# Three mixed sequence blocks in one kernel: other order of half slabs, sums, loads and banks around the first ups of two MLPs

## The reference

```python
# block 2
hdn = jnp.square(jax.nn.relu(rms_norm(x, mlp_norm_g) @ w_up))
x = x + hdn @ w_down
# block 3
x = layer_norm_3(ALPHA * x + jnp.square(jax.nn.relu(x @ w1)) @ w2, ln2_g, ln2_b)
```

## Time and profile before

| | |
|---|---|
| median of 3 runs | 3543.8 us (3541.1 to 3544.37) |
| the profiled execution | 3541.67 us |
| its span, first to last instruction | 3540.4 us |
| TensorE busy | 3437.9 us, 97% |
| VectorE, ScalarE, GpSimd busy | 2406.9, 1323.4, 1414.0 us |
| mean granted TensorE clock | 0.990 |

### The profile page before, as it was taken

One profiled execution on the slowest core, in us unless ns is written; L12 is line 12 of the kernel. 1 busy time (PEld: TensorE's weight loads), 2 busy tenths in 40 slices (PEclk: granted clock), 3 DMA queues, 4 the chain that ended last, 5 costly groups with the idle time before them and its releaser, 6 DMA issues.

```text
span 3540.4 us, 46507 instructions
## 1 busy us (share of the span) xinstructions
PE 3437.9 (97%) x17822; PEld 2839.0 (80%) x17822; DVE 2406.9 (68%) x3137; ACT 1323.4 (37%) x1950; POOL 1414.0 (40%) x916
## 2 busy tenths in 40 slices
PE   8999999999999999999979999999999979999997
PEld 7998888889888887887868877887777758887886
DVE  6677608999653474345488878777566668887786
ACT  5565522222231343443332234444322342234443
POOL 4444422232233451112465545445113455554443
PEclk9999999999999999999999999999999989999998
DMA  3111021111242341111434357544012243447552
GB/s 110 37 31 37 31 90 42 60 60 59 85 143 95 106 153 38 32 32 42 161 110 150 145 213 236 172 122 134 30 36 82 62 135 145 147 159 274 158 172 78
DMA packets 147532, 372.22 MB, mean 105 GB/s; under 512 B 16368, under 2 KB 16624, under 8 KB 147312
## 3 DMA queue, kind: packets, MB, share of 16 engines
q1 hardware_dynamic: 147312, 369.24, 31.1%
HBM read 280.05 MB, written 89.13 MB: 104 GB/s over the span
## 4 chain that ended last, share of the span: by engine, by line
PE 86%; DVE 7%; ACT 2%; DMA 2%; issue 2%; POOL 1%; SPq 0%; DVEq 0%; ACTq 0%
PE psum L669 48%; PE psum L1226 15%; PE psum L1245 14%; PE psum L825 1%; PE psum L1123 1%; PE psum L1090 1%; PE psum L1105 1%; POOL wl L3662 1%; DMA raw<-in_wdn 1%; PE psum L770 1%; POOL wl L3679 0%; DMA B<-keep_x 0%; PE psum L850 0%; PE psum L849 0%; DVE k L3362 0%
## 5 line engine op out<-in xcount | busy, mean ns | idle before, releaser
L3662 POOL TENSOR_TENSOR wl<-raw,wh 128x512 fp32r<-128x512 f32 x412 | 612.4, 1508 | 1316.5 <-ACT wh L1513 1316.5
L669 PE MATMUL psum<-hh,wh 128*128 128x512 f32 (+2 forms) x2864 | 920.7, 389 | 35.5 <-POOL wl L3662 31.2
L669 PE MATMUL psum<-hh,wl 128*128 128x512 f32 (+2 forms) x2864 | 881.5, 376 | 0.0
L669 PE MATMUL psum<-hl,wh 128*128 128x512 f32 (+2 forms) x2864 | 878.0, 375 | 0.0
L669 PEld LDWEIGHTS psum<-hh,wh 128*128 128x128 f32 x2864 | 510.7, 189 | 142.0 <-issue 54.1
L669 PEld LDWEIGHTS psum<-hl,wh 128*128 128x128 f32 x2864 | 526.4, 189 | 93.2
L669 PEld LDWEIGHTS psum<-hh,wl 128*128 128x128 f32 x2864 | 527.2, 189 | 86.5
L3679 POOL TENSOR_TENSOR wl<-wsum,wh 128x512 fp32r<-128x512 f32 x280 | 421.9, 1515 | 391.4 <-ACT wh L2081 391.4
L2081 ACT ACTIVATE wh<-wsum 128x512 fp32r<-128x512 f32 x280 | 176.7, 634 | 484.4 <-PE psum L1245 207.6
L1513 ACT ACTIVATE wh<-raw 128x1024 fp32r<-128x1024 f32 x206 | 217.3, 1055 | 271.7 <-PE psum L669 244.9
L2612 DVE SCALAR_TENSOR_TENSOR psum<-av,vec,psum 128x1024 f32<-128x1024 f32 x232 | 299.2, 1290 | 7.9
(11 more groups left out here) (517 smaller groups left out, 5070.7 us busy)
## 6 DMA issues: line engine op xcount, KB each, us to landing
raw<-in_wts SPq DMA_DIRECT2D x206, 512.0 KB, 3.6
keep_hidden<-B SPq DMA_DIRECT2D x168, 256.0 KB, 2.1
hh_f<-keep_hidden SPq DMA_DIRECT2D x100, 256.0 KB, 2.8
hl_f<-keep_hidden SPq DMA_DIRECT2D x96, 256.0 KB, 2.8
raw<-in_wup SPq DMA_DIRECT2D x28, 512.0 KB, 4.4
rawx<-in_wup SPq DMA_DIRECT2D x28, 512.0 KB, 4.3
raw<-in_wdn SPq DMA_DIRECT2D x56, 256.0 KB, 3.3
rawx<-in_wdn SPq DMA_DIRECT2D x56, 256.0 KB, 3.4
```

What stands on the lines that cost most here:

```text
L669: ins = pe.matmul(out, w, x[:, k, c0:c0 + width], start=first and n == only[0], stop=final and n == only[-1])
L3662: gp.tensor_tensor(wl[:, s, a], raw[:, s, a], fp(wh[:, s, a]), SUB).then_inc(*c.lo.tick(i, p))
```

## The change

- The half slabs run in the order of `FIRST_UPS`: q0 to q3 as before, then tile 2 and tile 3 for hf 1 on the slabs that are still in place (`HELD`), then tile 1 and tile 0 on two new slabs, base+4 and base+5. Each MLP has two slabs fewer; slab numbers move.
- Squares are made by ScalarE right behind the relu.
- VectorE makes the sums for products 4 and 1, five `w_add`s, then those for 7, 3 and 6. Between the sums and the low halves of products 1, 7, 3 and 6 it waits for GpSimd's low half of slab base+4, of slab base+5, and of the weights of n0 and n1. GpSimd asks for slab base+4 behind its last low half of the input, not before it.
- In MLP3 the addition of a bias to tiles of X on ScalarE (`offset`) goes by halves, four early ones among q0 to q3.
- The first pair of up blocks is loaded ahead of slabs base+4 and base+5, into `rawx`; pairs alternate the other way.
- At the seam the last pair's second row and its last four sums stand behind `act_low` of five different down steps (`last_hidden`), SyncE keeps them one by one, and X comes back by halves from step 11 on.
- After an MLP `aux` has four banks, where it had three and `head` one.

```diff
+FIRST_UPS = ((0, 0, 0), (1, 1, 0), (2, 2, 0), (3, 3, 0), (2, 2, 1), (3, 3, 1), (4, 1, 1), (5, 0, 1))
+HELD = (2, 3)
...
         def first_ups(base, ver):
-            for hf in range(2):
-                for u in range(4):
-                    gemm_half(base + 4 * hf + u, hf, c.ev("up", base, u, hf), ver if u == 0 else None)
-                side.drain()
+            for q, (i, u, hf) in enumerate(FIRST_UPS):
+                gemm_half(base + i, hf, c.ev("up", base, u, hf), ver if q % 4 == 0 else None, int(hf and i in HELD))
+                if q % 4 == 3:
+                    side.drain()
...
+            x = up_half(q)
+            se.activation(x, pairs.of(base + i, e)[:, hf, :], ACT.Relu).then_inc(*c.ev.tick("up", base, u, hf))
+            se.wait_ge(*c.ev("up", base, u, hf))
+            se.activation(x, x, SQUARE).then_inc(*c.ev.tick("squared", base, u, hf))
...
+        def first_ups(base, high, offset=None):
+            early, late = (((0, 4), (1,), (2,), (6,)), (0, 4, 1, 2, 6)) if offset else (((),) * 4, ())
+            for q, tiles in enumerate(((), (0, 1), (2, 3, 4), (5, 6, 7))):
+                if q in (1, 2):
+                    split(base + q + 1)
                 for k in tiles:
                     high(k, 1)
+                relu_half(base, q)
+                for k in early[q]:
+                    offset(k, 0)
+            for k in late:
+                offset(k, 1)
+            for q in range(4, 8):
+                if q < 6:
+                    se.wait_ge(*c.gemm(base + FIRST_UPS[q][0], 1))
+                    split(base + q)
+                relu_half(base, q)
+                if q < 7:
+                    in_highs(base, (4, 1, 7)[q - 4])
...
-        def in_sums(base, p):
+        def in_sums(base, p, middle=None):
...
+            if middle:
+                ve.wait_ge(*middle)
             for k in range(4):
                 ve.wait_ge(*c.in_hi(base, p, k))
...
+        def last_hidden(base, m):
+            j = PAIRS - 1
+            if m == 0:
+                ve.wait_ge(*c.post("21", base, j))
+                ve.wait_ge(*c.post("22++", base, j))
+                row_done(base, j, 1)
+            else:
+                sum_of(base, j, (3, 1, 4, 7)[m - 1])
...
         def fast_mlp(base):
-            for u in range(4):
-                squared(base, u, 0)
-            for u, p in enumerate((4, 1, 7)):
-                in_sums(base, p)
-                squared(base, u, 1)
-            for n in range(2):
+            in_sums(base, 4)
+            in_sums(base, 1, c.lo(base + 4, 1))
+            for n in range(5):
                 w_add(base, n)
-            squared(base, 3, 1)
-            for n in range(2, 5):
-                w_add(base, n)
-            in_sums(base, 3)
-            in_sums(base, 6)
+            in_sums(base, 7, c.lo(base + 5, 1))
+            in_sums(base, 3, c.w_lo(base, 0))
+            in_sums(base, 6, c.w_lo(base, 1))
...
         def fast_mlp(base, name):
+            up_pair(base, 0)
+            fetch(base + 5)
             for q in range(8):
...
+            last = {5: (2, 6), 6: (5,), 7: (3,), 8: (1,), 9: (4,), 10: (7,)}
+            back = [(4 * a + b, 1) for b in range(4) for a in range(2)] + [(k, 0) for k in range(KT)]
+            for m in range(NFAST - NUP):
                 down_step(base, m)
+                for p in last.get(m, ()):
+                    keep_block(base, PAIRS - 1, p)
+                if m == 11:
...
-            aux.only(*(psum[:, f[z], :] for z in (4, 5, 6)))
-            aux.freed = [fold_done(base, 6, j) for j in range(3)]
-            head.only(psum[:, f[7], :])
-            head.freed = [fold_done(base, 6, 3)]
+            aux.only(*(psum[:, f[z], :] for z in (4, 5, 6, 7)))
+            aux.freed = [fold_done(base, 6, j) for j in range(4)]
...
-                block(("up", base, j, z), (raw, rawx)[j % 2][:, s, :], A["wup"][which[base], 2 * j + z])
+                block(("up", base, j, z), (rawx, raw)[j % 2][:, s, :], A["wup"][which[base], 2 * j + z])
```

More of the change, by code:

```diff
@@ L434, in spent @@
     def spent(i):
-        return c.gemm(i, 1 if i in DOWN else 0)
+        return c.gemm(i, 1 if i in DOWN or i - MLP2 in HELD or i - MLP3 in HELD else 0)
     def free_tile(ver, k):
@@ L536, in w_block @@
             j = n // 7
-            return (raw, rawx)[j % 2][:, (mk[0] + base) % 2, 512 * mk[1]:512 * mk[1] + 512]
+            return (rawx, raw)[j % 2][:, (mk[0] + base) % 2, 512 * mk[1]:512 * mk[1] + 512]
         t = (n - NUP) % PAIRS
@@ L579, in slab_behind @@
     def slab_behind(i):
-        return next((m for m in (MLP2, MLP3) if i in (m + 8, m + 9)), None)
+        return next((m for m in (MLP2, MLP3) if i in (m + 6, m + 7)), None)
     def acc_of(st):
@@ L1209, in fast_mlp @@
                 if n == 0:
-                    for point in (*aux.freed, *head.freed):
+                    for point in aux.freed:
                         if point:
@@ L2124, in fast_mlp @@
                     first_high(base, m - 5 * PAIRS - 4)
-            split(base + 9)
+            split(base + 7)
         split(OUT2 + 3)
@@ L2356, in scalar @@
         half_root("v1", 1)
-        first_ups(MLP3, last_high, range(KT))
+        first_ups(MLP3, last_high, offset)
         fast_mlp(MLP3)
@@ L3081, in first_low, with row_done, sum_of @@
                              SUB).then_inc(*c.a_lo.tick("first", base, k, hf))
+        def row_done(base, j, m):
+            x = cbuf(j)[:, m, :]
+            ve.scalar_tensor_tensor(x, x, 0.0, x, MAX, MUL).then_inc(*c.post.tick(("row 0", "row 1")[m], base, j))
+            ve.wait_ge(*c.post(("row 0", "row 1")[m], base, j))
+        def sum_of(base, j, q):
+            a, op, b = IN_SUM[q]
+            if j == 0 and q == 6 and base == MLP3:
+                for k in range(KT):
+                    ve.wait_ge(*c.stored("xm3", k))
+            if j > 1:
+                ve.wait_ge(*c.kept(base, q, j - 2))
+            ve.tensor_tensor(hid_sum(j, q), hid_block(j, a), hid_block(j, b), op).then_inc(*c.post.tick(q, base, j))
+        def last_hidden(base, m):
[6 more added lines that the diff above has]
+                sum_of(base, j, (3, 1, 4, 7)[m - 1])
         def hidden(base, n):
@@ L3089, in add @@
                 ve.tensor_tensor(out, a, b, op).then_inc(*c.post.tick(key, base, j))
[L3091 to L3098, removed]
             if p in (2, 4):
@@ L3119, in hidden @@
                 ve.wait_ge(*c.post("11++", base, j))
-                x = cbuf(j)[:, 0, :]
-                ve.scalar_tensor_tensor(x, x, 0.0, x, MAX, MUL).then_inc(*c.post.tick("row 0", base, j))
-                ve.wait_ge(*c.post("row 0", base, j))
-                sum_of(6)
+                row_done(base, j, 0)
+                sum_of(base, j, 6)
             else:
@@ L3142, in fold @@
                 if FIRST_FOLD[mt] == p:
-                    ve.wait_ge(*c.loaded("xl", base, 4 * mt[0] + j))
+                    ve.wait_ge(*c.loaded("xl", base, 4 * mt[0] + j, mt[1]))
                 if FIRST_FOLD[mt] == p and base == MLP3:
@@ L3169, in fast_mlp @@
                     hidden(base, n)
+                elif m < 5:
+                    last_hidden(base, m)
                 if m >= PAIRS and t in (1, 3, 5, 7):
@@ L3675, in fast_mlp @@
         def fast_mlp(base):
-            split(base + 7)
+            split(base + 5)
             for n in range(NFAST):
@@ L3697, in half_lows @@
                 half_low(ver, 5, hf, src(5, hf))
-                split(first + 4 * hf + 4)
+                if not hf or ver not in ("ff2", "ff3"):
+                    split(first + 4 * hf + 4)
                 half_low(ver, 7, hf, src(7, hf))
@@ L3959, in fast_mlp @@
                             sp.wait_ge(*c.kept(base, p, j))
-                if 6 <= m < PAIRS:
-                    k = m - 6
-                    for key in [(name, k)] if k < 4 or base == MLP3 else [(name, k, hf) for hf in range(2)]:
+                if m >= 11 and back:
+                    k, hf = back.pop(0)
+                    for key in [(name, k)] if k < 4 or base == MLP3 else [(name, k, z) for z in range(2)]:
                         sp.wait_ge(*c.stored(*key))
-                    load(("xl", base, k), X[:, k, :], XS[k])
+                    load(("xl", base, k, hf), side_of(X[:, k, :], hf), side_of(XS[k], hf))
                 if 0 <= m - 5 * PAIRS < 8:
```

120 lines of the change are left out of this document (49 added, 71 removed).

## The result

The kernel after takes 3481.7 us (median of 4 runs, 3480.7 to 3483.4) against 3543.7 us for the kernel before on the same chip: a ratio of 0.983 (95% interval 0.981 to 0.984). It is 62 us faster. I had said 3507, and 3495 at the fastest: the sign was right, the size was 25 us short.

What follows compares the result with a forecast made beforehand. TensorE, busy 97% of the span, was taken as the bound, so only its idle time could go. Entries 29.5 plus seams 7.8 made 37.3 off 3541.67 or the median 3543.8: 3504.4 or 3506.5, said as 3507; range 3495 to 3524.

Steps and rivals of the forecast that it cites:

- zero, at most some tenths either way: Four banks in aux instead of three and one in head: same four waits before product 0, a little looser rotation; about zero.
- Entries: Start of the fast MLPs, q3's end to fifth product: 12.6 us gained in MLP2, 18.9 in MLP3, less 2; 29.5.
- the case in which slab base+5's piece gets in: MLP2's entry: GpSimd splits slab base+5 before q7 needs it, no q7 stall; 7.6 us left over, gain 14.6.
- the middle: MLP2's entry: 12.6 us, between gains of 14.6 and 10.6, as the sixth operation lies between the trace's rows.
- product 4's stall: Entries: product 4's pieces on GpSimd still meet VectorE's sums and lows of 6; 0.3 plus 2.4 us.
- product 0's two: MLP3's entry: stalls before product 0 for ScalarE's high half, 4.1 us, and GpSimd's low half, 1.8.
- for what I can't see: Allowance of 2 us taken off the gain of the two entries.
- Seams: From the fast ups to the downs: stalls of 2.0 and 1.9 us in each MLP go; 7.8, bounds 4.0 to 7.8.
- The fourth: Rival, rule as written: no GpSimd piece is held over one VectorE operation; gain 49.8 us, so 3494; chance 0.12.
- The forecast's own account of a hold: GpSimd pieces meeting an old VectorE run wait for its end, a young one, one operation; undecided between 4 and 7 operations.
- The second rival: Stalls move more than they go: base+5 held in both MLPs, product 0 later, one seam stall stays; 3519 or 3524; 0.20.
- The fifth: Rival, slower: holds move from slabs to weight pieces of products 0, 2 and 4 at the entries; 3553 us; 0.05.

## Why the prediction was 25 us short

The step that failed is the one that says of the banks "zero, at most some tenths either way". It measured 13.9 us in the trace, 13.1 and 15.4 in the two runs that swap it. I priced it where the text of the change has it, at the four waits ahead of product 0. But `aux` is set there for all that follows up to the next MLP, and the mLSTM takes a bank from it for every transpose, row spread and state product. `head` is taken only with the `lead` of block 1's projections, so in block 3 its bank lay idle. The first wait can be read off the code: gate columns, two transposes of v, then two row spreads are the first five takers. Of three banks the second spread gets the one that ScalarE must first copy v out of (3.59 us, `<-ACT v`); of four it gets that of the gate columns (0.75, `<-DVE eT`). I had the four waits of the mLSTM, 10.6 us, in the very view that the earlier trace rows is cut from, and left them out because no line of the diff lies in that stage. Bounds of "nothing" and "these 10.6 us" would have been a better forecast, 37.3 to 47.9, so 3496 at the far end. Even these would have been too small: the stage gave 13.9, as a wait also costs clock behind it, and the rest of the error is at the entries and seams.

**Entries.** 29.5 said, 35.4 measured. MLP2 gave 14.6, the figure of the case in which slab base+5's piece gets in. That it fits to the tenth is luck: the stalls came to 6.6 in place of 7.6, and the matmuls took 1.0 more than their worth, which this case had put at nothing. I had taken the middle between that and 10.6, for want of a row between the fourth and the seventh operation. MLP3 gave 20.8 for 18.9: product 4's stall came to 0.17 in place of 2.7, product 0's two to 3.51 and 0.64 in place of 4.1 and 1.8; the clock took 3.4 where I said 1. I had added clock and stalls as if they were independent; as shown above, what the clock took came out of product 4's stall, so their split says little and the sum is what counts. The 2 us "for what I can't see" weren't there. So 2.0 of the 5.9 is the middle, 1.9 MLP3's stalls, 2.0 the allowance.

**Seams.** 7.8 said, 10.3 measured, 4.3 and 6.0: the two pairs of stalls were 3.9 each and all went. The rest is mostly the 1.8 us of lower clock behind the second stall of MLP3, for which I had no term. The row in one piece is shown as the cause of the first stall; the cause of the second is argued.

Behind that 0.5 us is lost, mostly near the end. The kernel before has a stall of 1.4 us there (a slab's matmul behind VectorE) and the kernel after has none. Yet the same stretch of matmuls, from the end of a 2.77 us stall that both have, is 1.8 us longer in the kernel after, at a clock of 0.76, here before and after:

```profile
3496.42:3508.81 12.39, 10.73 (x61) 8.78 (x62) 8.01 (x16) 4.14 (x7) 3.53 (x3) 1.00 0.00 0
...
3434.93:3449.11 14.18, 13.78 (x61) 11.33 (x62) 8.01 (x16) 4.24 (x7) 3.52 (x3) 0.76 0.00 1
```

The runs with three banks, with four banks alone, with squares on VectorE and with X in whole tiles are like the kernel before there; the others have no such stall and take as long as the kernel after, or up to 1.4 us longer, and it follows no edit. Some of it comes back in the last matmuls, 1.1 us. The 1.9 us ahead of the change are of the same sort: the profiled runs of the ten kernels are some 4 us apart by then.

Together: 37.3 forecast, 13.9 banks, 5.9 entries, 2.5 seams, 1.9 ahead of the change, less 0.5 at the end: 61.0.

**The rivals.** The fourth gave 3494, nearest to the measured time, and is wrong all the same: it had every piece of GpSimd get in behind one operation, and without VectorE's waits a piece takes 11.36 us. A number that comes near isn't evidence for its mechanism. The Trainium skill ("SBUF — State Buffer", Summary: rules for kernel authors) has the second of the two blocked until the first finishes; this trace agrees only if a whole unbroken run of VectorE counts as the first, once GpSimd has not got in early.

The forecast's own account of a hold, by the age of VectorE's run, needs one correction: the age counts from GpSimd's last piece. In the kernel before VectorE had no pause from 1773.05 to 1800.77, and yet these two pieces, asked for in its eleventh operation since then, got in. GpSimd's last piece had ended 0.5 us earlier.

```profile
1785.30 3.47 POOL L3662 TENSOR_TENSOR wl<-raw,wh 128x512 fp32r<-128x512 f32 x2 [0.53 <-ACT wh L1513]
```

Counted in this way, the ten traces agree. Of GpSimd's low halves asked for while VectorE had more than 3 us of its run left, all up to the fifth operation got in (3.2 us at most). Each from the seventh operation on, 38 in all, ended 1.1 us after VectorE's run did. Whether operations or time decides they don't tell.

The second rival's "moves on" holds where one engine's order alone is changed (product 0's high half), not for the change as a whole. The fifth had the holds move from slabs to weight pieces: with the waits taken out just that happens, one per entry, 7.79 and 8.52 us, and it costs 15 us, far from the third held piece per entry from which I had it decide.

**What makes up the entries' 35.4 us.** VectorE's wait 15, weights in place 5 to 7, the squares 0 to 5. Each was taken out of the kernel after by itself, so that they simply add up isn't shown. The other 8 to 15 were not taken apart: the earlier split of base+4 and base+5, which the order of half slabs allows, and the order of the sums may stand behind them.

## What to carry to other kernels

A resource that an edit hands over (a bank, a buffer, a slot of a ring) is priced over its whole life: list every later taker up to the next hand-over, and look up the waits of that stage, however far from the diff. Where one engine's piece can be held by another's unbroken run, look for a place for it to get in: one wait per MLP, at which VectorE is idle for 1.2 us, was worth 15 us, two to three times the loads and splits that were saved. And the one stall that I tried to remove by an engine's order alone moved on to the next piece in that order.

## What the hardware showed that I had not expected

- GpSimd against a run of VectorE's two-input operations of 0.60 us: asked for in the fifth or sixth operation since its last piece, it got in (two pieces, 3.42 us); in the seventh and eighth it took 7.86 to 9.86 us, and in the sixteenth 11.36 us, till 1.1 us after the run's end, nine times its bare 1.28.
- The same stall ahead of product 0 (3.21 and 3.20 us) is followed by four matmuls in 1.17 us in one profiled run and 2.04 in another (kernel after, and the one with three banks). So the level of the clock behind a short stall differs between runs. In these entries it costs nothing, as a piece of GpSimd ends the next stall (17.08 and 17.07 us to that point); behind three stalls at the seams, and near the end, 1.8 us each were left.
- Bank rotation: with three banks in turn each taker waits for the engine that empties the bank of three takers back. One bank more moved that by one taker, and took 13 to 15 us from a stage of 342 and the stall ahead of it.
